# Seven sublayers on one core: warm-up matmuls and earlier transfers at the start, moved steps at a border, in the mLSTM and at the head of each feed-forward

## The chip, the cores and the metric

The kernel runs on one core of a Trainium2 chip. The metric is the time of one execution on the device, in microseconds (us); lower is better. The kernel before takes 1473.26 us, the median of 3 runs (1470.63 to 1473.32).

## What is computed

A stack of seven sublayers acts on x, 256 tokens by 1024 features in float32. Each has the same frame:

```
hmod = rms_norm(x, g_pre) * (1 + scale) + shift
x    = x + weight * gate * rms_norm(fn(hmod), g_post)
```

shift, scale and gate (1024 values each) are columns of `silu(c) @ ada_w + ada_b`, a modulation matrix of its own per sublayer. fn is in turn: feed-forward (n = 0), mLSTM (n = 1), feed-forward (2, 3), Mamba-2 (4), feed-forward (5), and a hybrid of attention and short convolution (6), after which a last rms_norm follows. The feed-forward is `(silu(h @ w1) * (h @ w3)) @ w2` with 2816 inner features. The mLSTM has four heads; its gates are prefix sums of log-sigmoids, and its scores are weighted with exponentials of differences of those sums, row maxima taken off. Some 335 MB of float32 weights are read once from HBM.

## The kernel before, in words

**Weights.** All weights come as 228 units of 1 MB (`units`, 128 x 2048 float32), consumed in a fixed order through a ring of five slots `raw`, `whi`, `wlo`. Each unit is loaded by SP (`load(u)`, line 244), rounded to `whi` by ScalarE (`hi(u)`, line 479), and its remainder written to `wlo` by VectorE (`lo(u)`, line 1546). A product is three passes: high by high, high by low, low by high (`three`, line 943 is the helper that issues every matmul). Slot u % 5 is free when TensorE has used the unit (`w_used`). A unit costs TensorE 24 matmuls of 512 columns.

**Modulation.** 84 further units (`ada_units`) hold the modulation matrices. VectorE multiplies each with silu(c) and sums along the row (`ada(v)`, line 1550, two instructions per unit). They pass through two slots (`araw`), and `load_ada(v)` on SP waits until VectorE is done with unit v - 2. SP is one queue in order: a `load_ada` that waits holds back every weight load behind it.

**First sublayer, start.** The modulation of n = 0 isn't there yet. Eight early modulation units 0 to 7 give one block of 128 features each. For blocks in `ON_PE` (0, 1, 2, 3, 7) the shift is a matrix-vector product on TensorE (`shift_column`, 8 matmuls with one moving column each, in plain float32, two records per matmul); else VectorE does it, and VectorE does every scale (`first_columns`). Then ScalarE modulates and rounds the block (`modulated_first`), VectorE writes its low part (`first_lo`), and TensorE multiplies it with the two tiles' weights (`first_products(b, k)`, 6 matmuls each). Weight units 0 to 3 serve these products. The sixth early modulation unit sits in slot 4 of `raw`, so `load(4)` waits until VectorE has used it (`e_used` >= 6); nine small loads for later sublayers follow it on SP.

**Feed-forward.** 11 tiles of 256 gated features. Tiles 0 and 1 (`first_two`) use units u to u+3 for token halves t = 0 and t = 1. Then tile i takes two up units and one down unit: in the loop for i = 2 TensorE uses units u+4, u+5 (up), u+6 (down), for i = 3 units u+7, u+8, u+9. `silu` (ScalarE, line 629) and `gate_up` (VectorE, line 1726) make the gated tile; `turn(i)` (TensorE, line 1143) transposes it; `gated_hi` (ScalarE, 633) and `gated_lo` (VectorE, 1732) split it. `turn(1)` waits for `gated_lo(0)`. The first product of tile 3 (unit u+7) waits for `gate_up(2, 0)`, since both use one PSUM bank. SP's order there is: load u+5, modulation v, load u+6, modulation v+1, load u+7, modulation v+2, load u+8, load u+9, modulation v+3. VectorE's order after the second token half's first `gate_up` is lo(u+5), ada(v), `gate_up(1, 1)`, lo(u+6), `gated_lo(0)`, ada(v+1), then in the loop lo(u+7), ada(v+2), `gated_lo(1)`, lo(u+8), `gate_up(2, 0)`. On ScalarE `gated_hi(0)` follows hi(u+6).

**Borders.** Between sublayers (`boundary`) the output of n is normalised and added to x (`gated_y`, `new_x`), x is normalised (`normed_x`), transposed on TensorE (`turn_x`), modulated and split (`modulated`, `split_x`), for token half 0 and then 1. The border behind the mLSTM is the only one with `late=True`.

**mLSTM.** Units u0 to u0+3 give values, u0+4 to u0+7 queries and keys (`feature_block`), u0+8 to u0+11 the output gate (`token_piece`), u0+12 to u0+15 the output projection (`down`). Between the feature blocks TensorE transposes gate rows to columns (line 1194), which waits for an exponential on ScalarE (line 677); VectorE copies them (`ml_cols`) ahead of lo(u0+9). `row_max` broadcasts row maxima. `turn_am(pair)` transposes the heads' output (line 1241), `turned_hi`/`turned_lo` split it for `down`.

The order of all instructions is written out by hand on each engine; there is no planner. The source that the change touches:

Of the kernel before, what the change touches and what calls it, by code (L numbers as in the profile page):

```python
# [13 lines left out]
P = 128  # L14
# [7 lines left out]
UNIT = 2048  # L22
# [57 lines left out]
def build(nc, x_in, units, ada_units, rows, cvec, fg_row, mlw, mlb, mbw, mbv, mbd, rel, onehot, negrow, ccol, out):  # L80
# [3 lines left out]
    with ctx:  # L84
# [54 lines left out]
        early = [araw[:, 0, :], araw[:, 1, :], m(4096, UNIT), ada_a[:, :], ada_b[:, :], raw[:, 4, :]]  # L139
# [99 lines left out]
        def _(sp):  # L239
# [44 lines left out]
            sp.wait_ge(S["e_used"], EARLY)  # L284
            load(4)
            sp.dma_start(oneh_sb[0:32, :], onehot[:, :]).then_inc(S["bias_in"], 16)
            sp.dma_start(negr_sb[0:H_AT, :], negrow[:, :]).then_inc(S["bias_in"], 16)
            sp.dma_start(rel_sb[0:32, :], rel[:, :]).then_inc(S["bias_in"], 16)
            sp.dma_start(mlw_sb[:, :, :], mlw).then_inc(S["mixer_in"], 16)
            sp.dma_start(mlb_sb[0:4, :], mlb[0:4, :]).then_inc(S["mixer_in"], 16)  # L290
            sp.dma_start(mlb_sb[32:36, :], mlb[4:8, :]).then_inc(S["mixer_in"], 16)
            sp.dma_start(mbw_sb[:, :, :], mbw).then_inc(S["mixer_in"], 16)
            sp.dma_start(mbv_sb[:, :], mbv).then_inc(S["mixer_in"], 16)
            sp.dma_start(mbd_sb[:, :], bass.AP(mbd.tensor, 0, [[0, P], [1, H_MB]])).then_inc(S["mixer_in"], 16)

            for n, kind in enumerate(KIND):
                u0 = FIRST[n]
                if kind == "ffn":
# [16 lines left out]
                    v += 2  # L315
                    for i in range(3, NF):
# [14 lines left out]
                        if i == 9:  # L331
                            gate_in(n)
                    load(down_unit(n, 9))
# [141 lines left out]
        def _(act):  # L475
# [35 lines left out]
            def first_two(n, evac, meanwhile=None):  # L511
# [14 lines left out]
                evac(1, 1, 7)  # L526
                hi(u + 6)
# [92 lines left out]
            for n, kind in enumerate(KIND):  # L620
                u0 = FIRST[n]
                if kind == "ffn":
                    b = NF * FFN_NO[n]

                    def silu(i, t, bank):

                        if b + i:
                            act.wait_ge(g_ok[t], b + i)
                        act.activation(sil[:, t, :], ps[:, bank, 0:FB], ACT.Silu).then_inc(sil_ok[t], 1)  # L629
# [6 lines left out]
                    if n == 5:  # L636
                        silu_c(1)
                    first_two(n, silu)
                    gated_hi(0)
# [13 lines left out]
                if kind == "ml":  # L653
# [60 lines left out]
                    for p in range(6, 8):  # L714
                        after_piece(p, u0 + 8, j0 + 2, ev_o)
                    turned_hi(1)
                    hi(u0 + 15)
# [223 lines left out]
        def _(pe):  # L941
# [42 lines left out]
            def feature_block(u, j, middle=None):  # L984
                for b in range(2):
                    free(b, j)
                    by_feature(u, 0, 2 * b)
                    r = by_feature(u, 0, 2 * b + 1)
                r.then_inc(w_used, 1)
# [81 lines left out]

            pe.wait_ge(S["const"], 4)
# [4 lines left out]
            for t in range(T):  # L1077
                turn_x(0, t)

            def shift_column(k):  # L1080
# [11 lines left out]
                for kk in range(KT):  # L1092
                    r = mm(ps[:, i % 2, 0:1], w[:, kk * P:(kk + 1) * P], cT[:, kk:kk + 1], start=(kk == 0), stop=(kk == 7))
# [18 lines left out]
            shift_column(0)  # L1112
            shift_column(1)
            first_products(0, 0)
            shift_column(2)
# [4 lines left out]
            for k in range(2, 5):  # L1120
                for b in range(2):
                    first_products(b, k)
            shift_column(7)
# [7 lines left out]
            for n, kind in enumerate(KIND):  # L1131
# [47 lines left out]
                if kind == "ml":  # L1179
# [10 lines left out]
                    pe.wait_ge(S["ml_rows"], 2)  # L1190
                    pe.wait_ge(S["ml_em"], 1)
                    for j, row in enumerate((8, 3)):
                        for t in range(T):
                            r = pe.transpose(ps[:, 0, 256 + (t * 2 + j) * 4:256 + (t * 2 + j) * 4 + 4],
                                             gt[0:4, row, t * P:(t + 1) * P], ident[0:4, 0:4])
                    r.then_inc(S["ml_ct"], 1)
# [7 lines left out]
                    feature_block(u0 + 6, j0 + 1, row_max)  # L1204
# [27 lines left out]
                    def turn_am(pair):  # L1232
# [3 lines left out]
                        for t in range(T):  # L1236
# [18 lines left out]
                    turn_am(0)  # L1255
                    token_piece(6, u0 + 8, j0 + 2)
                    token_piece(7, u0 + 8, j0 + 2)
                    for t in range(T):
                        for u in range(4):
                            if t == 0 and u == 2:  # L1260
                                turn_am(1)
                            pe.wait_ge(S["ml_lo"], 2 * (u // 2) + t + 1)
                            r = down(u0 + 12 + u, 2 * u, t, start=(u == 0), stop=(u == 3),
                                     middle=(lambda: turn_x(n + 1, 0)) if t and u == 3 else None)
# [268 lines left out]
        def _(dve):  # L1533
# [108 lines left out]
            def boundary(n, late):  # L1642
# [7 lines left out]
                if late:  # L1650
                    lo(u + 1)
# [3 lines left out]
                split_x(n + 1, 0, 1)  # L1655
                split_x(n + 1, 0, 2)
# [58 lines left out]
            for n, kind in enumerate(KIND):  # L1715
                u0 = FIRST[n]
                if kind == "ffn":
# [58 lines left out]
                if kind == "ml":  # L1776
# [83 lines left out]
                    def turned_lo(pair):  # L1860
                        for t in range(T):
# [416 lines left out]
```

## Time and profile before

| | |
|---|---|
| median of 3 runs | 1473.26 us |
| the profiled execution's own time | 1469.45 us |
| its span, first to last instruction | 1467.7 us |
| TensorE busy | 1415.7 us, 96% of the span |
| VectorE busy | 1013.3 us, 69% |
| ScalarE busy | 717.6 us, 49% |
| GpSimd busy | 92.2 us, 6% |
| mean granted TensorE clock | 0.993 |
| HBM read | 335 MB, 229 GB/s over the span |

Busy time of TensorE is the union of overlapping matmuls; at full clock a matmul of 512 columns has a record of 0.39 us, and one starts every 0.23 us. Line 943 is the helper through which all matmuls but the transposes are issued, so places are told apart by time and by tile names. In tile names `M` is one large working area that holds many arrays. Sublayers by time: n = 0 to 223 us, mLSTM to 345, n = 2 to 538, n = 3 to 729, Mamba-2 to 948, n = 5 to 1141, hybrid to the end.

### The profile page before, as it was taken

The page shows a single profiled execution, that of the slowest core. Times are in us where ns is not written, and L with a number is a line of the kernel's source. Part 1 is how long each engine was busy: PE and PEld are TensorE (multiplying, and loading weights), DVE is VectorE, ACT ScalarE, POOL GpSimd, SP SyncE. Part 2 cuts the span into 40 slices and gives each one's busy share as a digit, 9 for nine tenths or more (in the row PEclk, how much of TensorE's full clock was granted, in tenths as well). Part 3 has the DMA queues.
Part 4 walks back from the last instruction along what each step waited for, and adds up shares of the span by engine and source line. Part 5 has one row for each costly group of instructions (what it writes and reads, how often), then busy time and mean ns, then how long its engine had stood idle before and what let it go on. Part 6 is the DMA issues. An engine that isn't in the chain of part 4 may idle for free.

```text
span 1467.7 us, 18271 instructions
## 1 busy us (share of the span) xinstructions
PE 1415.7 (96%) x7478; PEld 1204.9 (82%) x7478; DVE 1013.3 (69%) x1239; ACT 717.6 (49%) x925; POOL 92.2 (6%) x112
## 2 busy tenths in 40 slices
PE   7999999998999999999999999999999999999997
PEld 6788887877788877888879978778888799999886
DVE  4887766876977767877668975678745544553765
ACT  5444346355544455444466676454334634454433
POOL 1000001002000010000010352100000100000000
PEclk9999999999999999999999999999999999999999
DMA  9788855853988747888545412478754454445542
GB/s 385 298 331 309 326 177 213 315 199 118 387 309 323 302 151 324 308 319 328 192 149 187 157 74 86 173 301 337 289 194 167 175 190 169 144 144 188 188 155 115
DMA packets 51395, 337.39 MB, mean 230 GB/s; under 512 B 6720, under 2 KB 9584, under 8 KB 11376
## 3 DMA queue, kind: packets, MB, share of 16 engines
q1 hardware_dynamic: 51312, 336.23, 61.4%
q8 instruction: 59, 0.97, 0.3%
q14 instruction: 24, 0.20, 0.0%
HBM read 335.12 MB, written 1.09 MB: 229 GB/s over the span
## 4 chain that ended last, share of the span: by engine, by line
PE 82%; DVE 6%; ACT 6%; DMA 3%; issue 2%; POOL 2%; SPq 0%; DVEq 0%; ACTq 0%; POOLq 0%
PE ps L943 79%; DVE wlo L1546 2%; DMA raw<-units 2%; ACT whi L479 2%; PE ps L1143 1%; POOL base L400 1%; ACT hf L553 1%; DVE hf L1932 1%; DVE x L1639 1%; PE ps L1051 1%; ACT M L544 1%; POOL ssx L401 1%; DMA cT<-ccol 0%; ACT M L536 0%; DVE M L1550 0%
## 5 line engine op out<-in xcount | busy, mean ns | idle before, releaser
L1546 DVE TENSOR_TENSOR wlo<-raw,whi 128x2048 fp32r<-128x2048 f32 x228 | 522.6, 2294 | 235.8 <-ACT whi L479 235.1
L943 PE MATMUL ps<-whi,xhi 128*128 128x512 f32 x1472 | 586.7, 399 | 14.5 <-DVE wlo L1546 8.8
L943 PE MATMUL ps<-whi,xlo 128*128 128x512 f32 x1472 | 576.3, 392 | 0.0
L943 PE MATMUL ps<-wlo,xhi 128*128 128x512 f32 x1472 | 576.2, 391 | 0.0
L479 ACT ACTIVATE whi<-raw 128x2048 fp32r<-128x2048 f32 x228 | 435.6, 1913 | 158.2 <-DMA raw<-units 158.1
L943 PEld LDWEIGHTS ps<-whi,xhi 128*128 128x128 f32 x1472 | 278.2, 189 | 78.4 <-issue 11.3
L943 PEld LDWEIGHTS ps<-whi,xlo 128*128 128x128 f32 x1472 | 278.0, 189 | 59.9
L943 PEld LDWEIGHTS ps<-wlo,xhi 128*128 128x128 f32 x1472 | 278.6, 189 | 55.0 <-issue 0.2
L943 PE MATMUL ps<-xhi,whi 128*128 128x256 f32 x704 | 203.3, 289 | 3.9 <-ACT M L868 3.9
L943 PE MATMUL ps<-xhi,wlo 128*128 128x256 f32 x704 | 200.6, 285 | 0.0
L943 PE MATMUL ps<-xlo,whi 128*128 128x256 f32 x704 | 200.6, 285 | 0.0
L1550 DVE SCALAR_TENSOR_TENSOR M<-M 128x1024 f32<-128x1024 f32 x158 | 186.9, 1219 | 0.0
L943 PEld LDWEIGHTS ps<-xhi,whi 128*128 128x128 f32 x704 | 136.4, 194 | 6.1 <-ACT M L868 4.9
L943 PEld LDWEIGHTS ps<-xlo,whi 128*128 128x128 f32 x704 | 136.5, 194 | 0.2
L943 PEld LDWEIGHTS ps<-xhi,wlo 128*128 128x128 f32 x704 | 136.4, 194 | 0.0
L400 POOL TENSOR_SCALAR base<-ssx 128x1 f32<-128x1 f32 x28 | 25.4, 907 | 1141.7 <-ACT M L544 796.7
L633 ACT ACTIVATE xhi<-ps 128x512 fp32r<-128x512 f32 x44 | 26.3, 597 | 134.1 <-PE ps L1143 134.1
L629 ACT ACTIVATE M<-ps 128x256 f32<-128x256 f32 x88 | 33.3, 383 | 98.9 <-PE ps L943 96.6
L1726 DVE TENSOR_TENSOR M<-M,ps 128x256 f32<-128x256 f32 x88 | 36.4, 418 | 30.0 <-ACT M L629 30.0
L1732 DVE TENSOR_TENSOR xlo<-ps,xhi 128x512 fp32r<-128x512 f32 x44 | 30.3, 689 | 27.3 <-ACT xhi L633 26.9
L868 ACT ACTIVATE M<-ps 128x512 f32<-128x512 f32 x28 | 16.6, 593 | 62.0 <-PE ps L943 61.9
L553 ACT ACTIVATE hf<-ps,shT,g1T 128x128 f32<-128x128 f32 x72 | 28.7, 448 | 35.0 <-PE ps L1051 35.0
(226 smaller groups left out, 853.3 us busy)
## 6 DMA issues: line engine op xcount, KB each, us to landing
raw<-units SPq DMA_DIRECT2D x228, 1024.0 KB, 4.9
M<-ada_units SPq DMA_DIRECT2D x81, 1024.0 KB, 7.1
gp<-gate_rows SPq DMA_DIRECT2D x7, 512.0 KB, 7.5
M<-cvec SPq DMA_DIRECT2D x2, 512.0 KB, 4.4
x<-x_in SPq DMA_DIRECT2D x1, 1024.0 KB, 6.0
ada_a<-ada_units SPq DMA_DIRECT2D x1, 1024.0 KB, 18.4
ada_b<-ada_units SPq DMA_DIRECT2D x1, 1024.0 KB, 22.4
raw<-ada_units SPq DMA_DIRECT2D x1, 1024.0 KB, 26.5
```

The lines of the kernel that those rows point to most:

```text
L400: step(pool.tensor_scalar(base[:, 0:1], a, b, EPS, ALU.add, ALU.add))
L401: pool.tensor_tensor(dst, base[:, 0:1], negh[:, 0:1], ALU.pow).then_inc(ready, 1)
L479: act.activation(whi[:, s, :], raw[:, s, :], ACT.Copy).then_inc(w_hi, 1)
L553: r = act.activation(hf[:, k, t_], ps[:, 2 * t + q // 2, (k % 4) * P:(k % 4 + 1) * P], ACT.Identity, scale=g1T[:, n, k:k + 1], bias=shT[:, ...
L629: act.activation(sil[:, t, :], ps[:, bank, 0:FB], ACT.Silu).then_inc(sil_ok[t], 1)
L633: act.activation(xhi[:, 8 + 2 * (i % 4):10 + 2 * (i % 4), :], ps[:, 6, :], ACT.Copy)\
L868: act.activation(hT[:, first + 4 * i + 2 * b:first + 4 * i + 2 * b + 2, :], ps[:, 4 + b, :].rearrange("p (a b) -> p a b", b=SEQ), func)\
L943: return pe.matmul(out, lhsT, rhs, start=start, stop=stop, skip_group_check=True)
L1546: dve.tensor_tensor(wlo[:, s, :], raw[:, s, :], whi[:, s, :].bitcast(F32), ALU.subtract)\
L1550: return dve.scalar_tensor_tensor(out=w, in0=w, scalar=1.0, in1=cb, op0=ALU.mult, op1=ALU.mult, accum_out=sums[:, column:column + 1])
L1726: dve.tensor_tensor(g[i % 2][:, t, :], sil[:, t, :], ps[:, bank, FB:2 * FB], ALU.mult)\
L1732: dve.tensor_tensor(xlo[:, j:j + 2, :], ps[:, 6, :].rearrange("p (a b) -> p a b", b=SEQ), xhi[:, j:j + 2, :].bitcast(F32), ALU.subtract).t ...
```

## The change

At the start, TensorE runs matmuls of the constant `ones` tile with itself into PSUM banks 7 and 2, whose results nobody reads; `shift_column` uses 128 equal moving columns instead of one. The sixth early modulation unit moves to `M`, so that `load(4)` waits for nothing, and in its place the first `silu` of n = 0 waits for VectorE to have used that unit. The small loads are moved behind the load of unit 6 (three of them) and into the loop at i = 9 (six). In every feed-forward ScalarE's `gated_hi(0)` goes ahead of hi(u+6); on VectorE `gate_up(1, 1)` and `gated_lo(0)` go ahead of lo(u+6), and both ada units behind it. For n = 5 ScalarE's silu of the second conditioning vector moves behind hi(u+5). At the border behind the mLSTM lo(u+1) goes behind the first two modulated quarters. In the mLSTM the transposes of gate rows move into the following feature block, VectorE's copy of them ahead of lo(u0+8), and `turn_am(1)` with its splits is done by token halves, lo(u0+15) between them.

```diff
-        early = [araw[:, 0, :], araw[:, 1, :], m(4096, UNIT), ada_a[:, :], ada_b[:, :], raw[:, 4, :]]
+        early = [araw[:, 0, :], araw[:, 1, :], m(4096, UNIT), ada_a[:, :], ada_b[:, :], m(12288, UNIT)]
@@ sync
-            sp.wait_ge(S["e_used"], EARLY)
             load(4)
-            sp.dma_start(oneh_sb[0:32, :], onehot[:, :]).then_inc(S["bias_in"], 16)
...
+            def bias_loads():
+                sp.dma_start(oneh_sb[0:32, :], onehot[:, :]).then_inc(S["bias_in"], 16)
...
+            def mixer_loads():
+                sp.dma_start(mlw_sb[:, :, :], mlw).then_inc(S["mixer_in"], 16)
...
@@ feed-forward loads
                     load_ada(v + 1)
                     v += 2
+                    if n == 0:
+                        bias_loads()
...
                         if i == 9:
                             gate_in(n)
+                            if n == 0:
+                                mixer_loads()
@@ scalar: first_two, silu, feed-forward
                 wait_used(act, u + 3)
                 evac(1, 1, 7)
+                if late:
+                    late()
                 hi(u + 6)
...
                         if b + i:
                             act.wait_ge(g_ok[t], b + i)
+                        else:
+                            act.wait_ge(S["e_used"], EARLY)
...
-                    if n == 5:
-                        silu_c(1)
-                    first_two(n, silu)
-                    gated_hi(0)
+                    first_two(n, silu, (lambda: silu_c(1)) if n == 5 else None, lambda: gated_hi(0))
@@ scalar: mLSTM
+                    hi(u0 + 15)
                     turned_hi(1)
-                    hi(u0 + 15)
                     hi(u0 + 16)
@@ tensor: feature_block, start
-            def feature_block(u, j, middle=None):
+            def feature_block(u, j, middle=None, early=None):
                 for b in range(2):
                     free(b, j)
                     by_feature(u, 0, 2 * b)
                     r = by_feature(u, 0, 2 * b + 1)
+                    if early and b == 0:
+                        early()
...
+            def keep_clock(bank, count):
+                for _ in range(count):
+                    mm(ps[:, bank, 0:P], ones[:, 0:P], ones[:, 0:P], start=True, stop=True)
+
+            pe.wait_ge(S["const"], 1)
+            keep_clock(7, 28)
             pe.wait_ge(S["const"], 4)
...
             r.then_inc(S["cols_tr"], 1)
-            for t in range(T):
-                turn_x(0, t)
+            keep_clock(7, 6)
+            turn_x(0, 0)
+            keep_clock(7, 2)
+            turn_x(0, 1)
...
-                    r = mm(ps[:, i % 2, 0:1], w[:, kk * P:(kk + 1) * P], cT[:, kk:kk + 1], start=(kk == 0), stop=(kk == 7))
+                    r = mm(ps[:, i % 2, 0:P], w[:, kk * P:(kk + 1) * P], cT[:, kk:kk + 1].to_broadcast([P, P]),
+                           start=(kk == 0), stop=(kk == 7))
...
             shift_column(0)
+            keep_clock(7, 4)
             shift_column(1)
+            keep_clock(7, 4)
             first_products(0, 0)
+            keep_clock(7, 3)
             shift_column(2)
...
-            for k in range(2, 5):
+            for k in (2, 3):
                 for b in range(2):
                     first_products(b, k)
+            pe.wait_ge(S["xt_ok"], 4)
+            keep_clock(2, 3)
+            for b in range(2):
+                first_products(b, 4)
@@ tensor: mLSTM
-                    pe.wait_ge(S["ml_rows"], 2)
-                    pe.wait_ge(S["ml_em"], 1)
...
+                    def turn_rows():
+                        pe.wait_ge(S["ml_rows"], 2)
+                        pe.wait_ge(S["ml_em"], 1)
...
-                    feature_block(u0 + 6, j0 + 1, row_max)
+                    feature_block(u0 + 6, j0 + 1, row_max, turn_rows)
...
-                    def turn_am(pair):
+                    def turn_am(pair, halves):
...
-                                turn_am(1)
+                                turn_am(1, (1,))
                             pe.wait_ge(S["ml_lo"], 2 * (u // 2) + t + 1)
+                            middle = None
+                            if (t, u) == (0, 1):
+                                middle = lambda: turn_am(1, (0,))
+                            if (t, u) == (1, 3):
+                                middle = lambda: turn_x(n + 1, 0)
@@ vector: boundary
                 normed_x(n + 1, 0)
-                if late:
-                    lo(u + 1)
                 modulated(n + 1, 2)
                 split_x(n + 1, 0, 0)
                 modulated(n + 1, 3)
                 split_x(n + 1, 0, 1)
+                if late:
+                    lo(u + 1)
@@ vector: feed-forward
                     gate_up(0, 1, 6)
                     lo(u0 + 5)
+                    gate_up(1, 1, 7)
+                    gated_lo(0)
                     if n == 5:
                         dve.wait_ge(S["c_ok"], 2)
+                    lo(u0 + 6)
                     ada(v)
-                    gate_up(1, 1, 7)
-                    lo(u0 + 6)
-                    gated_lo(0)
                     ada(v + 1)
@@ vector: mLSTM
-                    lo(u0 + 8)
-                    ada(v + 2)
                     dve.wait_ge(S["ml_ct"], 1)
                     dve.tensor_copy(colm[:, :, :], ps[:, 0, 256:272].rearrange("p (a b) -> p a b", b=8))\
                        .then_inc(S["ml_cols"], 1)
+                    lo(u0 + 8)
+                    ada(v + 2)
...
-                    turned_lo(1)
+                    turned_lo(1, (0,))
+                    lo(u0 + 15)
+                    turned_lo(1, (1,))
                     ada(v + 8)
-                    lo(u0 + 15)
                     ada(v + 9)
```

## Rows read from the trace of the kernel before

**Rows 1.** Waits of TensorE: engine, line, releaser; us in total, times, longest.

```profile
PE ps L943 <- DVE wlo L1546: 8.8, 7, 1.4
PE ps L1143 <- DVE xlo L1732: 3.3, 2, 3.0
PE ps L1143 <- issue: 2.9, 3, 1.6
PE ps L1194 <- ACT M L677: 2.5, 1, 2.5
PE ps L943 <- DVE xlo L1865: 2.0, 1, 2.0
```

**Rows 2.** Busy time by stretch: busy per engine, granted clock, DMA share, GB/s.

```profile
14.60:36.50 21.90, 21.90 (x85) 20.06 (x84) 14.48 (x22) 12.86 (x17) 0.00 (x0) 1.00 1.01 421
36.70:55.80 19.10, 19.10 (x93) 15.82 (x91) 14.31 (x25) 8.37 (x17) 0.00 (x0) 1.00 0.62 207
65.70:68.70 3.00, 3.00 (x16) 2.50 (x15) 3.00 (x5) 1.53 (x2) 0.00 (x0) 1.00 0.99 401
268.80:272.00 3.20, 3.20 (x17) 3.20 (x17) 3.20 (x5) 0.00 (x0) 0.00 (x0) 0.50 1.01 422
327.00:330.00 3.00, 3.00 (x8) 2.33 (x8) 3.00 (x8) 3.00 (x2) 0.00 (x0) 0.50 0.00 0
```

**Rows 3.** Timeline of TensorE, first sublayer: start, duration, operation, count, idle before.

```profile
14.45 6.83 PE L943 MATMUL ps<-cT,M 128*128 128x1 f32 x32
22.99 0.63 PE L943 MATMUL ps<-wlo,xhi 128*128 128x512 f32 x1
...
45.77 1.84 PE L943 MATMUL ps<-cT,M 128*128 128x1 f32 x16
...
65.33 0.63 PE L1143 MATMUL ps<-ident,M 128*128 128x128 f32 x4 [2.98 <-DVE xlo L1732]
```

**Rows 4.** First sublayer: timelines of SP, ScalarE, VectorE; the page's DMA issues.

```profile
6.63 0.46 SPq L277 DMA_DIRECT2D ada_b<-ada_units  x1
ada_b<-ada_units SPq DMA_DIRECT2D x1, 1024.0 KB, 22.4
28.68 1.89 ACT L479 ACTIVATE whi<-raw 128x2048 fp32r<-128x2048 f32 x1
34.78 0.43 DVE L1690 TENSOR_TENSOR xlo<-hf,xhi 128x256 fp32r<-128x256 f32 x1 [1.89 <-ACT xhi L606]
...
45.30 0.42 DVE L1690 TENSOR_TENSOR xlo<-hf,xhi 128x256 fp32r<-128x256 f32 x1
```

**Rows 5.** mLSTM sublayer: timelines of VectorE and TensorE.

```profile
279.70 0.48 DVE L1811 SCALAR_TENSOR_TENSOR hf<-ps,M,mask 128x256 f32<-128x256 f32 x1
291.78 1.02 PE L943 MATMUL ps<-M,hf 128*128 128x256 f32 x4
```

**Rows 6.** Timelines and chain: third sublayer's first tiles, and two mLSTM transfers.

```profile
375.69 0.39 ACT L629 ACTIVATE M<-ps 128x256 f32<-128x256 f32 x1 [3.64 <-PE ps L943]
376.69 0.33 SPq L255 DMA_DIRECT2D M<-ada_units  x1
386.75 1.92 ACT L479 ACTIVATE whi<-raw 128x2048 fp32r<-128x2048 f32 x1 [4.27 <-DMA raw<-units]
390.91 0.74 DVE L1726 TENSOR_TENSOR M<-M,ps 128x256 f32<-128x256 f32 x2
381.58 16.38 PE ps L943 x72
265.98 0.43 SPq L244 DMA_DIRECT2D raw<-units  x1
273.24 1.92 ACT L479 ACTIVATE whi<-raw 128x2048 fp32r<-128x2048 f32 x1 [5.43 <-DMA raw<-units]
```

**Rows 7.** ScalarE ahead of sixth sublayer's first tile; the page's group of L1550.

```profile
966.07 1.04 ACT L561 ACTIVATE M<-M 128x1024 f32<-128x1024 f32 x1
L1550 DVE SCALAR_TENSOR_TENSOR M<-M 128x1024 f32<-128x1024 f32 x158 | 186.9, 1219 | 0.0
```

More of the change, by code:

```diff
@@ L283, in _ @@
                 load_ada(v)
-            sp.wait_ge(S["e_used"], EARLY)
             load(4)
-            sp.dma_start(oneh_sb[0:32, :], onehot[:, :]).then_inc(S["bias_in"], 16)
[L287 to L294, printed above, removed]
+            def bias_loads():
+                sp.dma_start(oneh_sb[0:32, :], onehot[:, :]).then_inc(S["bias_in"], 16)
+                sp.dma_start(negr_sb[0:H_AT, :], negrow[:, :]).then_inc(S["bias_in"], 16)
+                sp.dma_start(rel_sb[0:32, :], rel[:, :]).then_inc(S["bias_in"], 16)
+            def mixer_loads():
+                sp.dma_start(mlw_sb[:, :, :], mlw).then_inc(S["mixer_in"], 16)
+                sp.dma_start(mlb_sb[0:4, :], mlb[0:4, :]).then_inc(S["mixer_in"], 16)
+                sp.dma_start(mlb_sb[32:36, :], mlb[4:8, :]).then_inc(S["mixer_in"], 16)
+                sp.dma_start(mbw_sb[:, :, :], mbw).then_inc(S["mixer_in"], 16)
+                sp.dma_start(mbv_sb[:, :], mbv).then_inc(S["mixer_in"], 16)
+                sp.dma_start(mbd_sb[:, :], bass.AP(mbd.tensor, 0, [[0, P], [1, H_MB]])).then_inc(S["mixer_in"], 16)
             for n, kind in enumerate(KIND):
@@ L509, in after_piece, with first_two @@
                     evac(1, i)
-            def first_two(n, evac, meanwhile=None):
+            def first_two(n, evac, meanwhile=None, late=None):
                 u = FIRST[n]
@@ L1189, in _ @@
                     feature_block(u0 + 4, j0)
-                    pe.wait_ge(S["ml_rows"], 2)
-                    pe.wait_ge(S["ml_em"], 1)
[L1192 to L1196, printed above, removed]
+                    def turn_rows():
+                        pe.wait_ge(S["ml_rows"], 2)
+                        pe.wait_ge(S["ml_em"], 1)
+                        for j, row in enumerate((8, 3)):
+                            for t in range(T):
+                                r = pe.transpose(ps[:, 0, 256 + (t * 2 + j) * 4:256 + (t * 2 + j) * 4 + 4],
+                                                 gt[0:4, row, t * P:(t + 1) * P], ident[0:4, 0:4])
+                        r.then_inc(S["ml_ct"], 1)
                     def row_max():
@@ L1230, in head @@
                         mm(d1, e2, ones[:, 0:1], stop=True).then_inc(S["ml_nd"], 1)
-                    def turn_am(pair):
+                    def turn_am(pair, halves):
                         if pair == 0:
                             pe.wait_ge(S["ml_den"], H_ML)
-                        for t in range(T):
+                        for t in halves:
                             pe.wait_ge(S["ml_am"], 4 * pair + 2 * t + 2)
@@ L1254, in _ @@
                     token_piece(5, u0 + 8, j0 + 2)
-                    turn_am(0)
+                    turn_am(0, (0, 1))
                     token_piece(6, u0 + 8, j0 + 2)
@@ L1260, in _ @@
                             if t == 0 and u == 2:
-                                turn_am(1)
+                                turn_am(1, (1,))
                             pe.wait_ge(S["ml_lo"], 2 * (u // 2) + t + 1)
-                            r = down(u0 + 12 + u, 2 * u, t, start=(u == 0), stop=(u == 3),
-                                     middle=(lambda: turn_x(n + 1, 0)) if t and u == 3 else None)
+                            middle = None
[3 more added lines that the diff above has]
+                                middle = lambda: turn_x(n + 1, 0)
+                            r = down(u0 + 12 + u, 2 * u, t, start=(u == 0), stop=(u == 3), middle=middle)
                             if t:
@@ L1858, in denominator, with turned_lo @@
                             mark(r)
-                    def turned_lo(pair):
-                        for t in range(T):
+                    def turned_lo(pair, halves):
+                        for t in halves:
                             dve.wait_ge(S["ml_hi"], 2 * pair + t + 1)
@@ L1884, in _ @@
                     after_piece(5, u0 + 8)
-                    turned_lo(0)
+                    turned_lo(0, (0, 1))
                     ada(v + 7)
```

## The prediction

> **What bounds the kernel now.** I read the list of waits of TensorE first, then busy time by stretch for its clock, then the timelines around each place the change touches. TensorE is the bound: it is busy 96% of the span, and what is idle comes in short waits [rows 1]. The largest kind, 8.8 us over seven waits for a low part of a weight unit, lies in the borders, and the change leaves most of it alone. A second loss can't be seen in busy time. In [rows 2] the engine is fully busy in two stretches inside the mLSTM at a granted clock of 0.50 (1.2 GHz), where a 512-column matmul starts every 0.43 us (the record is 0.63) instead of every 0.23. From 14.6 to 36.5 us the granted clock reads 1.00, but the records are 0.63 there too [rows 3]: I take the pitch, and so the low clock, as true. The whole start until 36.6 runs at 1.2 GHz; after a run of 512-column matmuls without a pause it goes to 2.4.
>
> **Start of the first sublayer.** Two shift columns (16 matmuls) took 6.83 us at the low clock, one (8 matmuls) 1.84 at the high one [rows 3]. So 128 moving columns instead of one cost nothing as long as loading plain float32 weights sets the pace, as the equal rate of one column shows; bounds 0 to 1.8 us per column at most, and I take 0. The warm-up matmuls before 9 us lie where TensorE waited for its first data anyway; the later 19 take some 0.2 us each, 4 us, and most fall into gaps that the faster matmuls open.
>
> If the clock is high from about 10 us on, the chain moves to transfers and VectorE. The block-4 modulation unit landed at 6.63 + 22.4 = 29.0 us [rows 4]; weight unit 2 is the transfer ahead of it, and at 421 GB/s [rows 2] 1 MB takes 2.5, so it landed at 26.5. Its conversion started only at 28.68 [rows 4], because ScalarE was held by a shift column still being computed. Now it starts at 26.5. From its start to the low part of block 5 at 45.30 + 0.35 it was 17.0 us, with one wait of 1.89 for a slow shift column in it [rows 4]; without that 15.1, so block 5 is ready at 41.6 us. Blocks 5, 6 and 7 follow as 36 matmuls of 0.2275 us (16.38 / 72, [rows 6]), 8.2 us: the first products end at 49.8 instead of 55.7. That is **5.9 us** gained; 3 if the clock falls back once or twice on the way.
>
> `load(4)` now lands near 40 us, so units 4, 5 and 6 are in time, and the small loads lie behind them. `turn(1)` waited 2.98 us for `gated_lo(0)` [rows 3]; with it ahead of lo(6) and ada, and unit 6 there, the wait is gone: **3.0 us**. In n = 3 the same wait of 0.3 goes (3.3 less 3.0, [rows 1]).
>
> **mLSTM.** Transposing the gate rows 2.8 us later (24 matmuls of 256 columns) covers the 2.5 us wait for the exponential [rows 1]. That wait was followed by the stretch at 0.50, 16 matmuls of 0.213 instead of 0.118: 1.5 us [rows 2]. VectorE then sets the place of the heads: its exponents start at 279.70 [rows 5] behind transfers and products that don't move; from there exponents (2.7), lo (2.2), ada (2.3) and the weighting of the first head (0.5) give 287.4, where TensorE started that head at 291.8 [rows 5]. So **4.3 us**, at least 2.5.
>
> `turn_am(1)` by halves takes most of 1.96 and the 1.02 behind it (one of the seven, [rows 1]) and the second stretch at 0.50 (8 matmuls, 1.6 us) from TensorE: 4.4 us. But VectorE is next. It still has two splits, two ada units and two low parts ahead of the border, and only its wait shrinks: y is gated 1.15 us earlier, and so is x normalised. TensorE waits some 2.4 us at `turn_x`. Worth **1.2 us**, between 0.5 and 4.4. Lo(u+1) behind the modulated quarters at this border moves the first product up by some 0.8 and `gated_y` back by as much relative to the normalised x; what ends last there is the low part of unit u+3 on VectorE, which keeps its distance. I take 0, bounds -1 and +1.
>
> **Sixth sublayer.** ScalarE's silu of 1.04 us [rows 7] stood ahead of the chain to `turn(0)`, which waited 1.12 of the 2.9 us in [rows 1]: **0.9 us**.
>
> Sum of what is gained: 5.9 + 3.0 + 0.3 + 5.5 + 0.9 = 15.6 us.
>
> **What the new order in the feed-forward costs.** ada(v) now comes after lo(u+6), and `load_ada(v+2)` on SP waits for it, with load u+8 queued behind. In n = 2 the last product of the first two tiles ends at 375.65; the silu at 375.69 follows, and SP issues `load_ada` at 376.69 [rows 6]. In the new order ScalarE runs silu, `gated_hi(0)`, hi(u+6) until 378.4; lo(u+6), 2.2 us (386.75 to 390.91 less 1.92, [rows 6]), ends at 380.6; ada(v), two of 1.22 less their overlap [rows 7], at 383.0. `load_ada` is issued 6.3 us later than before. By then the queue of transfers has drained (unit u+7 landed at 380.1), so the pair starts from rest: the only such pair in the trace, issued at 265.6 and 265.98, had its second landed at 273.24, 7.6 us after the first issue [rows 6]. Unit u+8 thus lands at 390.6 instead of 386.75. From its landing to the end of `gate_up(2, 0)` it is 390.91 + 0.37 - 386.75 = 4.5 us [rows 6]: 395.1. TensorE wants to begin unit u+7 two units behind 381.58, at 392.5, and waits for that very `gate_up`. **A new wait of 2.6 us.** Measured from the end of the first two tiles it is the same in n = 3 (2.5) and n = 5 (2.8). In n = 0 lo(5) stands in the way too: ada(8) ends at 59.6, unit 8 lands at 67.2, the tile is gated at 71.8, and TensorE is there at 67.5: 4.3 us. Nothing stands behind each wait that would make it up: before, the slack at this place was 392.5 - 391.3 = 1.2 us, and the following tiles are again set by TensorE. Together 12.2 us. Bounds: a landing 1 us earlier or later moves each by 1; none at all if the pair lands 2.6 us sooner.
>
> **The clock behind these waits.** After 2.98 us without a matmul at 62 us the clock stayed high (65.7 to 68.7, [rows 2]); after 2.51 at 265 us and after 1.96 with transposes ahead at 325 it was 0.50, at 1.5 us each. For four new waits of 2.5 to 4.3 I take two falls, 3.0 us; bounds 0 and 6.
>
> The Trainium skill, page "TensorE: Matmul & The Clock Gate", section "HAM oscillation", says that a matmul engine that idles for a transfer in each round is throttled again each time. By that rule all four waits cost their 1.5, and the profiled time would be 3 us above the sum below. The row at 65.7 us does not agree with it, the two stretches at 0.50 do.
>
> **The sum.** -15.6 + 12.2 + 3.0 = -0.4 us against the profiled execution's 1469.45. That execution lies 3.8 us under the median of the runs (1473.26), so I forecast 1472.9.
>
> **Rivals.**
>
> *A, the new waits don't arise.* Transfers from rest land sooner than the one pair shows, or VectorE reaches ada(v) earlier. For it: one single pair is my evidence, and at these places TensorE had 1.2 us of slack. Against it: the queue on SP is in order, and its issue at 376.69 follows ada(v) by 0.03 us. Time: 1473.3 - 15.6 = 1457.7; with half of each wait 1464.
>
> *B, slower: the start stays at the low clock.* The warm-up matmuls and transposes don't raise the clock, or it falls back for good before 36 us, since TensorE is waiting for transfers there. For it: four transposes and 16 more at 9 to 14.5 us did not raise it, nor did a pause-free mix of one-column and 512-column matmuls. Then the 5.9 goes and the waits stay: -0.4 + 5.9 = +5.5, 1478.8. It decides (slower than can be told from no change) once more than 3.3 of the 5.9 us are lost.
>
> The same page, section "Part 4: PE-mode transpose", says that transposes don't count as work for the clock. The row agrees as far as it goes; the change adds plain matmuls, so the rule leaves B where it is.
>
> *C, the mLSTM steps bring nothing.* VectorE's chain, not TensorE, sets the heads even before: then 5.5 is lost, 1478.4 with all else as forecast. Against it: between VectorE's exponents at 279.70 and the first head at 291.8 lie 12.1 us, of which I count 7.7 as work [rows 5].
>
> **How the numbers follow.** A difference under 0.2% (2.9 us) can't be told from no change. My forecast has 62%: in it the number of clock falls and the landing times move the time by some 4 us either way (own range 1468 to 1478), so 20% faster, 31% within 0.2%, 11% slower. A has 22%, nearly all faster (21, and 1 the same). B has 9% and C 4%, 10 slower and 3 the same between them; 3% is left for what I don't name, split evenly. In all 42% faster, 36% the same, 22% slower. The range 1459 to 1479 leaves out the full case A and the worst of B.
>
> **What would show it.** Records of the 512-column matmuls before 36 us at 0.39 instead of 0.63, and the first products ending near 50 us: the start is right. No wait at line 1194, and the first head near 287 on the old scale: the mLSTM. A wait for VectorE's gated tile of line 1726 at the head of unit u+7 in all four feed-forwards, 2.5 to 4.3 us long, with `load_ada` issued 6 us later than before: the heart of the forecast. If that wait isn't there, the forecast is wrong and the time is near 1458.

## The result: 0.4% slower

The changed kernel takes **1477.4 us** in the median of 18 runs (1471.4 to 1484.0), the kernel before 1472.9 (18 runs, 1466.5 to 1478.7); the ratio is 1.004, 95% interval 1.0021 to 1.0058. The forecast was 1472.9, no change; the range of 1459 to 1479 holds the time, and a slower kernel had been given 22%. One execution is left out of all that follows, 3603 us for the kernel of experiment 2, whose other five took 1486 to 1492. The profiled execution took 1477.66, against 1469.45 before: 8.2 us, of which part is chance (below).

Waits of TensorE in the changed kernel, in the columns of [rows 1] (lines moved: 1546 to 1579, 1143 to 1170, 1865 to 1898, the gated tile's 1726 to 1759, the matmul helper's 943 to 951):

```profile
PE ps L951 <- DVE M L1759: 15.4, 4, 4.8
PE ps L951 <- DVE wlo L1579: 8.4, 7, 1.5
PE ps L1170 <- issue: 2.0, 3, 1.6
PE ps L951 <- DVE xlo L1898: 0.6, 1, 0.6
```

A kind that wasn't there leads the list: TensorE waits four times, 15.4 us, for the gated tile. The wait for the exponential (2.5) is gone, the 3.3 at `turn` for the gated low part is gone, and 2.0 for the mLSTM's turned rows has become 0.6.

The start, in TensorE's timeline (start, duration, operation, count, idle before). The warm-ups, then `turn(0)` of the first feed-forward, which before began at 56.23 (by experiments 2 and 6 that was late, see below):

```profile
1.08 9.24 PE L951 MATMUL ps<-ones 128*128 128x128 f32 x56 [1.08 <-POOL negh L386]
...
50.74 0.63 PE L1170 MATMUL ps<-ident,M 128*128 128x128 f32 x4 [0.34 <-DVE M L1759]
```

**The new wait.** The same place in n = 2 and n = 3 from the timelines of SP, ScalarE, VectorE and TensorE. SP issues `load_ada(v+2)` and behind it unit u+8; ScalarE converts it when it has landed; VectorE splits it and gates the tile; TensorE has waited for that tile. Of the two loads in the second line the first is unit u+8. Compare [rows 6]:

```profile
375.29 0.33 SPq L255 DMA_DIRECT2D M<-ada_units  x1
375.66 0.91 SPq L244 DMA_DIRECT2D raw<-units  x2
384.04 1.91 ACT L486 ACTIVATE whi<-raw 128x2048 fp32r<-128x2048 f32 x1 [9.38 <-DMA raw<-units]
385.98 2.29 DVE L1579 TENSOR_TENSOR wlo<-raw,whi 128x2048 fp32r<-128x2048 f32 x1 [2.88 <-ACT whi L486]
388.19 0.75 DVE L1759 TENSOR_TENSOR M<-M,ps 128x256 f32<-128x256 f32 x2
388.66 0.50 PE L951 MATMUL ps<-whi,xhi 128*128 128x512 f32 x1 [3.92 <-DVE M L1759]
...
573.28 0.33 SPq L255 DMA_DIRECT2D M<-ada_units  x1
580.73 1.91 ACT L486 ACTIVATE whi<-raw 128x2048 fp32r<-128x2048 f32 x1 [6.66 <-DMA raw<-units]
585.35 0.80 PE L951 MATMUL ps<-whi,xhi 128*128 128x512 f32 x1 [4.76 <-DVE M L1759]
```

**The clock behind it.** Busy time by stretch, in the columns of [rows 2] (the granted clock is the third figure from the end): behind every one of the four waits it is 0.50 to 0.52, that is 1.2 GHz. The mLSTM stretch, 0.50 in [rows 2], is at full clock:

```profile
72.00:75.00 3.00, 3.00 (x8) 2.32 (x9) 3.00 (x3) 0.45 (x1) 0.00 (x0) 0.50 1.00 423
265.00:285.00 20.00, 18.43 (x118) 16.01 (x117) 18.72 (x30) 8.20 (x6) 0.00 (x0) 1.00 0.98 401
389.00:392.00 3.00, 3.00 (x9) 2.31 (x8) 3.00 (x2) 0.52 (x1) 0.00 (x0) 0.52 1.03 431
585.70:589.70 4.00, 4.00 (x10) 3.12 (x10) 4.00 (x4) 1.11 (x1) 0.00 (x0) 0.50 1.01 422
1000.50:1003.50 3.00, 3.00 (x8) 2.32 (x8) 3.00 (x2) 0.49 (x1) 0.00 (x0) 0.50 1.01 429
```

The price of one low stretch can be read between two starts: from the first matmul of unit 7 to the next `turn` TensorE takes 5.6 us at full clock (72.76 to 78.32 in the kernel of experiment 7, shown there). In the changed kernel it takes 7.16, 7.17, 7.99 and 7.13:

```profile
71.73 0.80 PE L951 MATMUL ps<-whi,xhi 128*128 128x512 f32 x1 [3.52 <-DVE M L1759]
78.89 0.60 PE L1170 MATMUL ps<-ident,M 128*128 128x128 f32 x4
...
593.34 0.60 PE L1170 MATMUL ps<-ident,M 128*128 128x128 f32 x4
```

That is 1.6, 1.6, 2.4 and 1.5, together 7.1 us.

### The profile page after: what moved, and what is told of

It is laid out like the page before. It is cut to its first block, busy times and chain, and to the rows that moved or that the text cites. A ratio compares the mean times of both kernels' runs of the same rounds, so it can differ in the third digit from the quotient of the medians.

```text
span 1475.9 us, 18473 instructions
## 1 busy us (share of the span) xinstructions
PE 1421.8 (96%) x7578; PEld 1208.6 (82%) x7578; DVE 1014.1 (69%) x1239; ACT 716.9 (49%) x925; POOL 91.6 (6%) x112
## 4 chain that ended last, share of the span: by engine, by line
PE 74%; DVE 9%; DMA 6%; ACT 6%; issue 3%; POOL 2%; SPq 0%; DVEq 0%; POOLq 0%; ACTq 0%
PE ps L951 71%; DMA raw<-units 6%; DVE wlo L1579 3%; ACT whi L486 3%; DVE M L1583 2%; PE ps L1170 1%; POOL base L407 1%; DVE hf L1966 1%; DVE x L1672 1%; ACT M L553 1%; ACT hf L562 1%; PE ps L1061 1%; POOL ssx L408 1%; ACT M L545 0%; PE ps L1431 0%
## 5 line engine op out<-in xcount | busy, mean ns | idle before, releaser
L951 PE MATMUL ps<-whi,xhi 128*128 128x512 f32 x1472 | 587.8, 399 | 29.2 <-DVE M L1759 15.4
```

The lines of the kernel that those rows point to most:

```text
L951: return pe.matmul(out, lhsT, rhs, start=start, stop=stop, skip_group_check=True)
```

## The experiments

Theory: the order of the feed-forward alone makes the kernel slower, through SP. `load_ada(v+2)` can't be issued before `ada(v)` has freed its buffer; `ada(v)` now runs late, unit u+8 is queued behind it, and TensorE, held up by the late tile, also loses its clock. Rivals: the late release matters less than the rate of the transfers (R); VectorE's own load, with another split ahead of the tile, is what comes late (V). All ratios are to the kernel before, run beside them on the same chip. The experiments ran on three chips, so they are compared by these ratios; the interval behind a ratio is its 95% interval. The edits are shown in short: `...` stands for what is left out, and a wait of n = 5 that moves along with `ada(v)` isn't shown.

**1. Feed-forward order undone, all else kept.** VectorE's calls stand as before, and so does `gated_hi(0)` on ScalarE:

```diff
     lo(u0 + 5)
-    gate_up(1, 1, 7); gated_lo(0); lo(u0 + 6); ada(v); ada(v + 1)
+    ada(v); gate_up(1, 1, 7); lo(u0 + 6); gated_lo(0); ada(v + 1)
```

> The changed kernel with its feed-forward order undone on ScalarE and VectorE (gated_hi(0) behind hi(u+6); ada(v) ahead of gate_up(1,1), gated_lo(0) behind lo(u+6)); start, mLSTM, border and the moved silu of n = 5 stay. Theory Q (the queue): the late ada(v) holds load_ada(v+2) on SP, and load u+8 behind it. Then the four waits at the head of unit u+7 (3.5, 3.9, 4.8, 3.2 us in the profile, 15.4 together) and the low clock behind them (30 matmuls at 0.43 instead of 0.23, 6 us) go, and a wait at turn(1) of n = 0 comes back, 1 to 3 us: 18 to 20 us less than the changed kernel, near 1459 us, ratio to the kernel before 0.990. Rival R (rest): the loss is in the start, the mLSTM or the border, and the feed-forward order is worth its turn(1) wait: then this is no faster than the changed kernel, 1477 to 1480.

Measured: 1462.6, ratio **0.9932** (0.9909 to 0.9955). The four waits are gone, and the old one is back, with seven low-clock matmuls behind it. So the rest of the change is worth 0.7%. The expectation was 18 to 20 us under the changed kernel; it is some 15, and `turn` now waits 4.9 us for the gated low part, in three places, where the kernel before had 3.3:

```profile
61.24 0.75 PE L1171 MATMUL ps<-ident,M 128*128 128x128 f32 x4 [2.99 <-DVE xlo L1766]
```

**2. Feed-forward order alone, on the kernel before.**

```diff
     lo(u0 + 5)
-    ada(v); gate_up(1, 1, 7); lo(u0 + 6); gated_lo(0); ada(v + 1)
+    gate_up(1, 1, 7); gated_lo(0); lo(u0 + 6); ada(v); ada(v + 1)
```

> The kernel before with nothing but the feed-forward order of the change on ScalarE and VectorE. Theory Q: four waits for gate_up(2,0) at the head of unit u+7, some 15 us together, and up to 6 us of low clock; less 3.3 us at turn(1): 1473 + 17 = 1490 us, ratio 1.011. Rival R: no such loss, turn(1)'s 3.3 us gained, 1470, ratio 0.998. Rival V (VectorE is simply full there, the transfer is not it): waits too, but unit u+8 lands before VectorE asks for it.

Measured: 1488.2 (median of five), ratio **1.0108** (1.0084 to 1.0132), as expected. Waits of its TensorE; behind each of the four, 6 to 13 matmuls at the low clock:

```profile
PE ps L944 <- DVE M L1727: 13.1, 4, 4.4
```

**3. ada(v) first.** The changed kernel with one call moved on VectorE:

```diff
     lo(u0 + 5)
+    ada(v)
     gate_up(1, 1, 7); gated_lo(0)
     lo(u0 + 6)
-    ada(v)
     ada(v + 1)
```

> The changed kernel with ada(v) alone moved back between lo(u+5) and gate_up(1,1); gated_lo(0) stays ahead of lo(u+6) and gated_hi(0) ahead of hi(u+6). Theory Q: load_ada(v+2) is issued at its old place, as soon as before, so all four waits and the low clock go, and turn(1) waits at most 1 us in n = 0: 1457 us, ratio 0.989, as fast as or 1 to 2 us faster than the kernel with the whole order undone. Rival V: early tile work is what delays the rest; at least half of the waits stay, 1468 or more.

Measured: 1457.7, ratio **0.9902** (0.9877 to 0.9927): some 20 us less than the changed kernel, by moving one call, two reductions of 1.2 us each. Its timelines in n = 2, the same four places as above:

```profile
366.68 0.33 SPq L255 DMA_DIRECT2D M<-ada_units  x1
367.05 4.38 SPq L244 DMA_DIRECT2D raw<-units  x2
375.50 1.92 ACT L486 ACTIVATE whi<-raw 128x2048 fp32r<-128x2048 f32 x1 [3.12 <-DMA raw<-units]
380.17 0.75 DVE L1759 TENSOR_TENSOR M<-M,ps 128x256 f32<-128x256 f32 x2
```

The issue comes 4.4 us after `turn(0)` (362.26) instead of 10.7, unit u+8 lands 13.2 us after it instead of 19.5, and the tile is gated at 380.17 + 0.42, before TensorE is there. Of the four waits one is left, 0.9 us in n = 0. V has fallen: VectorE does the same work ahead of that tile as in the changed kernel, in another order. R has fallen as well, at this place: unit u+8 lands 8.8 us after the issue of the modulation unit ahead of it (366.68 to 375.50), as slowly as in the changed kernel (8.75), and nobody waits for it.

**4. Weights first.** The changed kernel; SP issues unit u+8 ahead of the modulation unit:

```diff
     load(up_unit(n, i, 0))
+    if i == 3: load(up_unit(n, i, 1))
     load_ada(v)
-    load(up_unit(n, i, 1))
+    if i > 3: load(up_unit(n, i, 1))
```

> The changed kernel with its VectorE order untouched; on SP, for tile 3 alone, load u+8 goes ahead of load_ada(v+2). Theory Q: unit u+8 is loaded as soon as its slot is free, hi(u+8) is early, but ada(v+2) still lands late and stands ahead of lo(u+8) on VectorE: waits of some 1 us instead of 3 to 5, and most of the low clock gone, 11 to 17 us less: 1460 to 1466 us, ratio 0.992 to 0.995. Rival V: the queue is not it; unchanged, 1477.

Measured: 1463.2, ratio **0.9943** (0.9922 to 0.9964). VectorE's late `ada(v)` is kept, and some 70% of the loss that experiment 3 takes away is gone: what made the weights late is the queue on SP. The waits shrink to 6.6 us, and only one low stretch (7 matmuls) is left:

```profile
PE ps L954 <- DVE M L1762: 6.6, 4, 2.8
```

**5. The start alone, on the kernel before** (early block 5, the loads moved behind it, warm-ups, 128 columns):

```diff
-    sp.wait_ge(S["e_used"], EARLY)
     load(4)
+    keep_clock(7, 28)   ...
-    r = mm(ps[:, i % 2, 0:1], ..., cT[:, kk:kk + 1], ...)
+    r = mm(ps[:, i % 2, 0:P], ..., cT[:, kk:kk + 1].to_broadcast([P, P]), ...)
```

> The kernel before with only the edits of the first sublayer's start (early block 5 and the loads behind it moved, warm-up matmuls, 128 moving columns); the orders of mLSTM, border and feed-forward are those of before. Theory (the start is worth what it showed in the changed kernel, where turn(0) of n = 0 came 5.5 us earlier): turn(0) at 50.7 +- 0.5, turn(1) still waits some 3.0, all else shifted; time 5.5 to 6 us under before, ratio 0.996. Rival (the earlier start is taken back: ScalarE or SP are late at the first loads of the feed-forward, since they come no earlier): turn(0) early, but new waits up to unit 7 of n = 0, less than 3 us left, ratio above 0.998.

Measured: 1469.1, ratio **0.997** (0.9952 to 0.9988). `turn(0)` comes at 50.82, 5.4 us earlier, and `turn(1)` waits 3.00 as before. Behind that wait the clock falls here, which it didn't in [rows 2], and takes 1.3 back: from there up to the mLSTM the lead is 4.1. Expected were 5.5 to 6 us of time; the ratio gives 4.4 +- 2.7, which holds both that and a good deal less.

**6. mLSTM and border alone, on the kernel before.**

```diff
-    pe.wait_ge(S["ml_rows"], 2) ... transposes
-    feature_block(u0 + 6, j0 + 1, row_max)
+    feature_block(u0 + 6, j0 + 1, row_max, turn_rows)
-    turn_am(1)
+    turn_am(1, (0,)) ... turn_am(1, (1,))
```

> The kernel before with only the edits of the mLSTM (gate rows transposed later, turn_am by halves) and of the border behind it (lo(u+1) later). Theory: the wait for the exponential goes and the first products of n = 2 come 4.4 us earlier, as in the changed kernel (9.7 for products there less 5.5 and more from the stages before, by unit u+3 4.4); time 4 to 6 us under before, ratio 0.997. Rival (VectorE's chain sets the heads anyway): less than 1.5 us, ratio 0.999 or more, heads at the same place relative to VectorE's exponents.

Measured: 1466.5, ratio **0.9948** (0.9932 to 0.9965). Between the border of n = 0 and `turn(0)` of n = 2 its trace is 4.0 us shorter than before (149.85 to 145.81), as the theory had it; the runs give 7.7 +- 2.5, more than the theory's 4 to 6, though the interval reaches it.

**7. Clock held.** The changed kernel, and in each feed-forward, ahead of the new wait:

```diff
+    if i == 3:
+        keep_clock(7, 14)
     pe.wait_ge(g_ok[0], b + (i if i > 2 else 1))
```

> The changed kernel, and TensorE runs 14 more 128-column matmuls of ones (3.0 us by the rate of its warm-ups at the high clock) in each feed-forward ahead of its wait for gate_up(2, 0); nothing else is changed. Theory (the 15.4 us of waits and the clock behind them are two terms): the wait gets shorter by what the dummies take, the end of the wait stays where it is or moves by under 0.5, and the 30 matmuls behind the four waits run at the high clock, 6 us less: 1471 to 1472, ratio to before 0.999 to 1.000. Rival (the low clock costs nothing, since the order of transfers sets the next tiles too): the slow matmuls are gone and the time stays within 2 us of the changed kernel's, ratio 1.002 or more.

Measured: 1469.2, ratio **0.9978** (0.9962 to 0.9995), against 1.004 for the changed kernel: 0.6%, some 9 us, for work whose result nobody reads. Expected were 6 us (0.999 to 1.000). The dummies and the first matmul behind them in n = 0, and the clock there:

```profile
69.05 3.29 PE L951 MATMUL ps<-ones 128*128 128x128 f32 x28
72.76 0.50 PE L951 MATMUL ps<-whi,xhi 128*128 128x512 f32 x1 [0.42 <-DVE M L1761]
78.32 0.60 PE L1170 MATMUL ps<-ident,M 128*128 128x128 f32 x4
...
72.00:78.00 6.00, 5.58 (x26) 4.52 (x26) 5.98 (x9) 2.45 (x2) 0.00 (x0) 1.00 1.02 426
```

Seen from `turn(0)`, the tile of n = 0 is gated as late as in the changed kernel (20.6 us after it, 20.5 there). The low stretches are gone, 7.1 us by the changed kernel's trace; so the waits themselves and the clock behind them are two separate costs. In n = 2 and n = 3 the tile also came 1.3 and 2.3 us earlier in this execution, by faster landings. No more than one execution shows that, and nothing ties it to the dummies.

**8. No warm-ups.** The kernel of experiment 3 without `keep_clock` and with one moving column:

```diff
-    keep_clock(7, 28)   (and the six other calls)
-    r = mm(ps[:, i % 2, 0:P], ..., cT[:, kk:kk + 1].to_broadcast([P, P]), ...)
+    r = mm(ps[:, i % 2, 0:1], ..., cT[:, kk:kk + 1], ...)
```

> The changed kernel with ada(v) moved back between lo(u+5) and gate_up(1, 1), and without the warm-up matmuls and with one moving column in the modulation and shift products: what is left of the start's edits are the earlier transfers and the order. Compared with the same kernel with warm-ups (ratio 0.990). Theory (the start's 5.5 us come from the clock): the matmuls before 36 us run at the low clock again, turn(0) of n = 0 comes 4 to 5.5 us later than there (near 56), 1462, ratio 0.993 to 0.994. Rival (they come from the earlier transfers, weight unit 4 above all): turn(0) stays near 51 and the ratio near 0.990.

Measured: 1459.1, ratio **0.9912** (0.9886 to 0.9939). In the trace the theory holds: `turn(0)` at 55.09 instead of 51.22, 3.9 us later, and the 512-column matmuls before 36 us have records of 0.63 again. In time the two kernels can't be told apart (0.9902 against 0.9912, each +- 0.0025), so it is shown for the trace alone. The trace also shows something that [rows 3] doesn't. Without warm-ups the two shift columns took 4.01 us here, where [rows 3] has 6.83:

```profile
14.78 4.01 PE L951 MATMUL ps<-cT,M 128*128 128x1 f32 x32
```

So the clock rose near 14.5 us, with nothing but transposes ahead of it, and fell again before 19 us; from 19 to 34 us the profile grants 0.50. Experiments 2 and 6, with the start of the kernel before, show the same (4.11 and 3.96 us).

**9. Both remedies**, 3 and 4 together:

```diff
+    ada(v)                                   # VectorE, behind lo(u + 5)
+    if i == 3: load(up_unit(n, i, 1))        # SP, ahead of load_ada(v)
```

> The changed kernel with both remedies: ada(v) back between lo(u+5) and gate_up(1, 1) on VectorE, and SP issuing unit u+8 ahead of load_ada(v+2). Theory (one cause, the late issue of unit u+8 behind ada(v); either remedy takes the same wait away, so the two don't add): within 2 us of the kernel with ada(v) first alone, 1456 to 1459, ratio 0.989 to 0.992; the wait of 0.91 left there at unit 7 of n = 0 goes. Rival (two causes, the release of SP and the rate of the pair from rest, each with its own share): the two add, and the time is 5 us or more under that kernel, 1452 or less. Rival on the other side: the later modulation units come late for the next products that need them, and some of the gain is lost, above 1461.

Measured: 1462.1, ratio **0.9933** (0.9912 to 0.9954): the remedies don't add, which fits one cause; the rival of two causes (1452 or less) has fallen. Together they are if anything worse than 3 alone (0.9933 against 0.9902, with intervals that overlap), as the rival on the other side had it. In this trace the modulation unit is now the late one. VectorE waits for it, and TensorE for the tile behind it:

```profile
567.25 1.23 DVE L1586 SCALAR_TENSOR_TENSOR M<-M 128x1024 f32<-128x1024 f32 x1 [0.74 <-DMA M<-ada_units]
...
572.82 0.50 PE L954 MATMUL ps<-whi,xhi 128*128 128x512 f32 x1 [1.72 <-DVE M L1762]
```

**10. Border order undone**, on the kernel of experiment 3: `lo(u+1)` ahead of the modulated quarters.

```diff
+    if late: lo(u + 1)
     (normalised and modulated quarters)
-    if late: lo(u + 1)
```

> The changed kernel with ada(v) back between lo(u+5) and gate_up(1, 1), and at the border behind the mLSTM lo(u+1) ahead of the modulated quarters as before. The prediction put the change's order at 0, bounds -1 and +1. Theory: the first product of n = 2 comes up to 0.8 earlier or later than in the kernel with the change's order (turn(0) of n = 2 at 362.3 there, +-1), the time within 1.5 us, ratio 0.989 to 0.992. Rival (the order of the border, not the mLSTM's transposes, brought a good part of the 4 us there): turn(0) of n = 2 is 2 us or more later, near 365, ratio 0.992 or more.

Measured: **1454.4** (four executions), ratio **0.9888** (0.987 to 0.9906), the lowest of all, though not to be told from experiment 3 (0.9902 +- 0.0025). From the transposes of x to `turn(0)` of n = 2 it takes 27.63 us; the kernel of experiment 3 takes 28.80 for it (333.46 to 362.26), the one before 27.58, the changed one 28.78. All eight kernels with the change's order take 28.8 or 28.9 us, all four with the order of before 27.5 to 27.7. So the change's order at this border costs 1.2 us of trace, whatever else a kernel has:

```profile
333.11 1.09 PE L1061 MATMUL ps<-ident,M 128*128 128x128 f32 x8 [1.93 <-DVE M L1639]
344.29 2.28 DVE L1579 TENSOR_TENSOR wlo<-raw,whi 128x2048 fp32r<-128x2048 f32 x1
360.74 0.63 PE L1170 MATMUL ps<-ident,M 128*128 128x128 f32 x4 [1.59 <-issue]
```

The middle line is the low part of unit u+3, 11.2 us behind the transposes of x. In the kernel of experiment 3 it is 12.4 (333.46 to 345.84):

```profile
345.84 2.29 DVE L1579 TENSOR_TENSOR wlo<-raw,whi 128x2048 fp32r<-128x2048 f32 x1
```

## Why the prediction was wrong

Its mechanism was right at nearly every place. Two terms of the sum, the clock behind the waits and the waits, were too small, and one, the border, was put at nothing. Point by point, by what the two profiled executions show:

| step | forecast | measured |
|---|---|---|
| start | -5.9 | -5.5 (56.23 to 50.74; 5.4 alone) |
| `turn(1)`, n = 0 and n = 3 | -3.3 | -3.3 (the waits are gone) |
| mLSTM | -5.5 | -5.6 (border of n = 0 to transposes of x, 122.3 to 116.7) |
| border, lo(u+1) later | 0 (-1 to +1) | +1.2 |
| silu_c in n = 5 | -0.9 | -0.9 |
| four new waits | +12.2 | +15.4 |
| clock behind them | +3.0 | +7.1 |
| sum | -0.4 | +8.4 (the spans differ by 8.2) |

**The step that failed most is the clock behind the waits:** "For four new waits of 2.5 to 4.3 I take two falls, 3.0 us; bounds 0 and 6." The clock fell behind all four, at 1.5 to 2.4 each, 7.1 us. The one row that spoke for less was the 2.98 us wait at 62 us in [rows 2], after which the clock stayed high. At the same place the same wait comes back in experiments 1, 5 and 6 (2.99, 3.00 and 2.99 us): in 1 seven and in 5 four matmuls behind it ran at the low clock, in 6 none. So that row was one draw, not a rule, and I had given it as much weight as the two stretches at 0.50. Over all kernels here, of 15 waits of 1.7 to 4.8 us in the feed-forwards' first tiles 11 were followed by the low clock. What decides it stays open. In the runs, holding the clock is worth some 9 us (experiment 7, +- 4), against the 3.0 of the sum. The Trainium skill, page "TensorE: Matmul & The Clock Gate", section "HAM oscillation", was weighed against that row and set aside; its rule, that an engine idling for a transfer each round is throttled each time, agrees with this trace at all four places, though not with every wait: after 2.83 us in experiment 4 (576.61), 2.99 in experiment 6 and 1.72 in experiment 9 the clock read 1.00.

**The four waits.** Forecast and measured: 4.3 and 3.5, 2.6 and 3.9, 2.5 and 4.8, 2.8 and 3.2. The chain up to SP was exact in n = 2: `load_ada` 10.7 us after `turn(0)`, 10.8 by the forecast. The pair from rest landed 7.4, 8.75, 7.45 and 7.25 us after its first issue, where one pair had given 7.6; the 8.75 makes n = 2 late. In n = 3 the pair was not the cause: unit u+6 landed 6.3 us after `turn(0)`, in experiment 7 it was there by 4.2, so `ada(v)` and the issue came 2.1 later. Each is one late landing, and both waits are over the bound of 1 us that I gave a place. In experiment 2 the four waits sum to 13.1, so part of the 15.4 is this execution's. In n = 0 TensorE came 0.7 us later than forecast, and so waited less.

**The border.** "I take 0, bounds -1 and +1": its order costs 1.2 us in every trace. The first product of n = 2 does come 0.8 earlier, as forecast, but the low part of unit u+3, which was to keep its distance, comes 1.2 later (experiment 10), and TensorE waits for it.

**Where the numbers came out by luck.** For the start I forecast 5.9, and the two profiles show 5.5. But the trace of before was a late draw: with the same start `turn(0)` comes at 54.82 in experiment 2 and 54.55 in experiment 6, and in the eight kernels with warm-ups at 50.7 to 52.1. By the means (55.2 and 51.2) the start is worth 4.0. The row that B rests on (transposes and shift matmuls at 9 to 14.5 us "did not raise it") was the same single draw: in the three other kernels without warm-ups the clock rose there, for some 3 to 4 us (experiment 8). The mLSTM's 5.5 against 5.6 hides two misses that cancel: the first head came 3.6 us earlier, counted from the border (69.4 to 65.8), not 4.3, and the rest brought 2.1, not 1.2; its wait at `turn_x` was 1.9, not 2.4.

**Rivals.** A fell: the waits arise, in experiment 2 as well. B fell: the start runs at full clock. C fell: the mLSTM brought its 5.5.

**The sum against the median.** I added the difference to the median of three runs. The profiled execution of before had a mean granted clock of 0.993; the 61 executions of that kernel beside the experiments average 0.988. So profile against profile (8.2) puts the change's cost higher than the runs do, and the runs decide: 4.5 by the medians, 5.9 by the ratio (3.1 to 8.5). The parts run alone add up: -4.4 (start), -7.7 (mLSTM and border) and +15.9 (feed-forward order) make +3.8, each +- 2.5 to 3.5.

What is shown: the feed-forward order costs 1.1% alone and is what makes the change slower (1, 2, 3); the path is SP's queue behind `ada(v)` (3, 4); the clock is a separate term (7). The border's +1.2 (10), and that the start's gain comes from the clock (8), rest on traces without a difference in time that can be told.

## What to carry to other kernels

Before a step is moved later on one engine, look at who frees what: here two reductions of 1.2 us held a buffer, the buffer held a DMA issue, and the in-order issue queue held the weights of the next tile. The price was some 20 us (the changed kernel against experiment 3) for one such call of 2.4 us in each of four feed-forwards. A new wait on TensorE is priced with the clock behind it: here 11 of 15 had one. One place in one execution doesn't settle what the clock does there; several executions do. Where such a wait can't be avoided, filling it with matmuls nobody reads is worth trying.

## What the runs showed of the hardware

**One stretch carries much of the spread between executions.** At the end of the Mamba heads (64-column matmuls, with waits of 0.3 to 0.9 us) the clock falls in some executions for nearly 20 us, in some for a few and in some not at all. The same work, between two transposes, in the kernel of experiment 8 (884.48 to 898.85, clock 0.50) and in that of experiment 3 (878.15 to 887.67, clock 1.00):

```profile
885.00:890.00 5.00, 5.00 (x24) 4.32 (x22) 2.03 (x3) 2.93 (x8) 1.49 (x1) 0.50 0.01 3
890.00:895.00 5.00, 5.00 (x24) 4.52 (x23) 2.79 (x6) 2.37 (x7) 0.00 (x0) 0.50 0.00 0
895.00:900.00 5.00, 5.00 (x26) 5.00 (x26) 1.99 (x3) 2.07 (x2) 0.00 (x0) 0.50 0.00 0
```

```profile
878.00:883.00 5.00, 5.00 (x41) 4.21 (x40) 4.02 (x6) 3.64 (x11) 3.41 (x2) 1.00 0.00 0
883.00:888.00 5.00, 4.02 (x33) 3.58 (x33) 4.30 (x8) 3.50 (x6) 0.00 (x0) 1.00 0.01 3
```

It takes 14.4 us there and 9.5 here, and the two kernels don't differ at that place. Over the 18 runs of the changed kernel the time follows the mean granted clock: 1471.4 at 0.994, 1484.0 at 0.981. Why the clock falls there in one execution and not in the next stays open; no run tried to hold it.

**Matmuls of ones raise the clock.** With 28 of them from 1.08 us on, in 9.2 us in which TensorE had waited for its first data, the first 512-column matmuls have records of 0.39 to 0.47 us; before they had 0.63 [rows 3], and without them they have it again (experiment 8). The granted clock that the profile shows can miss this: it reads 1.00 from 14.6 to 36.5 us in [rows 2] and 0.50 from 19 to 34 us in experiment 8, and both traces have the same records of 0.63 there.
